# Four edits in a two-layer hybrid encoder: matmul order in the state-space mixer, a sum of squares on VectorE, and the order of the final norm

## The reference, cut to what matters

```python
def mamba2_mixer(h, in_proj, conv_w, conv_b, dt_bias, a_log, d_skip, norm_w, out_proj):
    proj = h @ in_proj                       # z | x, B, C | dt
    z, xbc, dt_raw = ...
    xbc = silu(causal_dwconv(xbc, conv_w) + conv_b)
    xs, b_mat, c_mat = ...                   # 8 groups: x 256 wide, B and C 128 wide
    y = ssd_scan(xs, dt, a, b_mat, c_mat)    # needs C.B scores, decays, x * dt
    y = (y + d_skip * xs) * silu(z)
    yg = y.reshape(bsz, seq, 8, 256)
    yg = yg * rsqrt(mean(yg * yg, axis=-1, keepdims=True) + RMS_EPS)
    return (yg.reshape(bsz, seq, 2048) * norm_w) @ out_proj

# the end of the kernel
    return rmsnorm(h, final_norm)            # h * rsqrt(mean(h*h) + eps) * w
```

## Time and profile before

| | |
|---|---|
| median of three executions | 1324.3 us |
| the profiled execution | 1324.34 us |
| its span, first to last instruction or transfer | 1322.5 us |
| TensorE matmul busy | 1078.8 us, 82% |
| VectorE busy | 480.3 us, 36% |
| ScalarE busy | 239.7 us, 18% |
| HBM read | 459.38 MB, a mean of 348 GB/s over the span |
| chain that ended last | TensorE 54%, DMA 36%, VectorE 5% |

### The profile page before, as it was taken

One profiled execution on the slowest core, in us unless ns is written; L12 is line 12 of the kernel. 1 busy time (PEld: TensorE's weight loads), 2 busy tenths in 40 slices (PEclk: granted clock), 3 DMA queues, 4 the chain that ended last, 5 costly groups with the idle time before them and its releaser, 6 DMA issues.

```text
span 1322.5 us, 22258 instructions
## 1 busy us (share of the span) xinstructions
PE 1078.8 (82%) x9526; PEld 728.6 (55%) x9531; DVE 480.3 (36%) x1244; ACT 239.7 (18%) x539; POOL 7.8 (1%) x29
## 2 busy tenths in 40 slices
PE   8999888756897576889999999987866787768576
PEld 7888644433554243547888888854434353425243
DVE  2341563322232222236665556465322222213233
ACT  2220111111111111113433334121111111111111
POOL 1000000000000000000000000000000000000000
PEclk9999978878797787789999999998887879878788
DMA  9754799999999999994656663489999999999995
GB/s 341 222 251 191 283 428 425 426 426 428 425 428 425 425 428 426 426 368 137 215 189 224 215 207 143 160 358 427 425 428 425 427 426 424 427 427 427 426 426 238
DMA packets 90109, 461.95 MB, mean 349 GB/s; under 512 B 17180, under 2 KB 56344, under 8 KB 63384
## 3 DMA queue, kind: packets, MB, share of 16 engines
q1 hardware_dynamic: 89648, 460.34, 85.9%
q10 hardware_dynamic: 360, 0.15, 0.0%
HBM read 459.38 MB, written 1.08 MB: 348 GB/s over the span
## 4 chain that ended last, share of the span: by engine, by line
PE 54%; DMA 36%; DVE 5%; issue 2%; ACT 1%; SPq 1%; POOL 0%; POOLq 0%; DVEq 0%
DMA w_gu<-in_expert_w_up 19%; DMA w_x<-in_expert_w_up 17%; PE pb L1377 10%; PE pa L1377 7%; PE pa L1615 6%; PE wa L1615 6%; PE acc L1401 4%; PE pb L1606 4%; PE wb L1624 4%; PE acc L1503 2%; PE pb L1593 2%; PE acc L1634 1%; PE pb L1432 1%; ACT arena L511 1%; PE pb L1668 1%
## 5 line engine op out<-in xcount | busy, mean ns | idle before, releaser
L1615 PE MATMUL pa<-w_gu,arena 128*32 128x256 f32 x1408 | 114.2, 496 | 67.6 <-DMA w_gu<-in_expert_w_up 64.7
L1128 DVE TENSOR_SCALAR lower<-lower 128x128 f32<-128x128 f32 x64 | 14.4, 225 | 397.9 <-ACT lower L511 397.9
L1615 PEld LDWEIGHTS pa<-w_gu,arena 128*32 128x32 f32 x1408 | 55.2, 142 | 128.4 <-DMA w_gu<-in_expert_w_up 72.8
L1615 PE MATMUL wa<-w_gu,arena 128*32 128x256 f32 x1536 | 101.4, 423 | 29.7 <-DMA w_gu<-in_expert_w_up 29.7
L1377 PE MATMUL pb<-hnT,w_x 128*128 128x256 f32 x496 | 109.9, 380 | 2.4 <-DVE arena L1203 2.4
L511 ACT ACTIVATE arena<-wb 32x256 f32<-32x256 f32 (+2 forms) x248 | 93.5, 377 | 98.3 <-PE wb L1624 91.3
L1606 PE MATMUL pb<-arena,hs 128*128 128x128 f32 x480 | 78.9, 332 | 31.0 <-issue 18.0
L1377 PEld LDWEIGHTS pb<-hnT,w_x 128*128 128x128 f32 x496 | 93.4, 190 | 15.0 <-issue 2.8
L1606 PEld LDWEIGHTS pb<-arena,hs 128*128 128x128 f32 x480 | 72.7, 239 | 45.4 <-issue 44.5
L1615 PEld LDWEIGHTS wa<-w_gu,arena 128*32 128x32 f32 x1536 | 51.6, 122 | 79.6 <-DMA w_gu<-in_expert_w_up 37.5
L1593 PE MATMUL pb<-arena 32*128 32x512 f32 x128 | 75.2, 668 | 14.7 <-DVE arena L1024 11.3
(11 more groups left out here) (332 smaller groups left out, 1300.7 us busy)
## 6 DMA issues: line engine op xcount, KB each, us to landing
w_gu<-in_expert_w_gate SPq DMA_DIRECT2D x44, 2048.0 KB, 31.9
w_gu<-in_expert_w_up SPq DMA_DIRECT2D x44, 2048.0 KB, 36.6
w_dn<-in_expert_w_down SPq DMA_DIRECT2D x32, 2048.0 KB, 41.1
w_x<-in_expert_w_gate SPq DMA_DIRECT2D x20, 2048.0 KB, 32.8
w_x<-in_expert_w_up SPq DMA_DIRECT2D x20, 2048.0 KB, 37.6
arena<-in_expert_w_down SPq DMA_DIRECT2D x16, 2048.0 KB, 38.1
hnT<-in_expert_w_down SPq DMA_DIRECT2D x16, 1024.0 KB, 36.5
arena<-in_expert_w_down SPq DMA_DIRECT2D x16, 1024.0 KB, 40.1
```

Of the source, the lines that this page charges most:

```text
L1128: link(v.tensor_scalar(eg, eg, 1.0, None, ALU.add))
L1615: ins = mm(gu[32 * j:32 * j + 32, :, :], xb[:, k, c0:c0 + CAP], w_gu[s][:, :, k, P * j:P * j + P], start=(k == 0), stop=(k == KC - 1))
```

## The change

1. **Order in units 0 and 1.** `odd_bc(g + 2)` stands right behind `odd_y(g)`, ahead of `odd_x(g + 1)`, for g = 0 and 1. From unit 2 on it stays behind `odd_ss(g)`.
2. **Order in the last unit.** In unit 7 `odd_z` stands ahead of `odd_scores`.
3. **Squares.** VectorE adds the two halves of the squares (128x256) in every unit, and `odd_ss` is one matmul, not two.
4. **Final norm.** VectorE multiplies the second half of the first tile by the norm's weights without the inverse root; ScalarE multiplies it by the inverse root afterwards, and that part is stored first. The mean of the second tile is formed ahead of the first scaling.

```diff
@@ SyncE, the stores
-            for n, (t, i) in enumerate(norm_parts()):
-                sp_.wait_ge(S["y_ready"], n + 1)
+            for t, i, sem, n in ((0, 1, "sum_sq", 2 * TT + 1), (0, 0, "y_ready", 2), (1, 0, "y_ready", 3), (1, 1, "y_ready", 4)):
+                sp_.wait_ge(S[sem], n)
@@ ScalarE, behind the four squares
+            act.wait_ge(S["y_ready"], 1)
+            act.wait_ge(S["rstd"], TT + NORMS - 1)
+            af(y_out[:, 0, 512:], y_out[:, 0, 512:], ACT.Copy, scale=st[:, 4, 0:1]).then_inc(S["sum_sq"], 1)
@@ VectorE, odd_gate
-                v.tensor_tensor(sq, yz, yz, ALU.mult).then_inc(S["yz_done"], 1)
+                link(v.tensor_tensor(sq, yz, yz, ALU.mult))
+                v.tensor_tensor(sq[:, 0, :], sq[:, 0, :], sq[:, 1, :], ALU.add).then_inc(S["yz_done"], 1)
@@ VectorE, the end
             mean_square(0)
             dve.wait_ge(S["fnorm_in"], 16)
-            dve.wait_ge(S["rstd"], TT + 4)
+            v.tensor_tensor(y_out[:, 0, 512:], h[:, 0, 512:], fnorm[:, 512:], ALU.mult).then_inc(S["y_ready"], 1)
+            mean_square(1)
+            dve.wait_ge(S["rstd"], TT + NORMS - 1)
             normed(0, 0)
-            mean_square(1)
-            normed(0, 1)
-            dve.wait_ge(S["rstd"], TT + 5)
+            dve.wait_ge(S["rstd"], TT + NORMS)
             normed(1, 0)
             normed(1, 1)
@@ TensorE, odd_ss
-                for j in range(2):
-                    ins = mm(wb[:, 0:SEQ], ones[:, :], sq[:, j, :], start=(j == 0), stop=(j == 1))
-                ins.then_inc(S["yss_done"], 1)
+                mm(wb[:, 0:SEQ], ones[:, :], sq[:, 0, :], start=True, stop=True).then_inc(S["yss_done"], 1)
@@ TensorE, the units
-                odd_scores(g)
-                odd_z(g)
+                if g == ODD_UNITS - 1:
+                    odd_z(g)
+                    odd_scores(g)
+                else:
+                    odd_scores(g)
+                    odd_z(g)
                 odd_y(g)
+                if g < 2:
+                    odd_bc(g + 2)
...
-                if g + 2 < ODD_UNITS:
+                if 2 <= g < ODD_UNITS - 2:
                     odd_bc(g + 2)
```

## The result

The changed kernel takes 1341.18 us (median of 4 executions, 1339.76 to 1341.88) against 1324.39 us for the kernel before (4 executions, 1322.28 to 1325.58). The ratio is 1.0128, with a 95% interval of 1.0116 to 1.0140: it is slower, by 16.8 us. Predicted were 1339.2 us, in a range of 1332.5 to 1343.5. The profiled execution took 1340.69 us with a span of 1338.9 us, 16.4 us more than before.

The account below looks back on a forecast made before the run. TensorE was taken to bound mixer C and the weight stream the experts, so mixer time delays the end. 10.0 + 4.0 - 1.7 + 1.5 + 1.7 - 0.6 = +14.9 us on 1324.34 gave 1339.2 us, range 1332.5 to 1343.5.

Parts of the forecast that it names:

- What bounds: TensorE bounds mixer C, the weight stream layer 1's experts; a microsecond more in mixer C ends the kernel a microsecond later.
- Edit 1, +10.0: Units 0 and 1: B/C no longer covers the silu of x, so scores start 7.0 us behind x; +10.0 us.
- The clock, +4.0: Behind the two 6.6 us gaps in mixer C TensorE's clock falls: 2.0 us twice, +4.0, bounds 2.6 and 6.0.
- the ten waits that I had read: TensorE waits of 2.9 to 8.3 us, all losing clock time behind them: 1.3 to 3.0 us, on average 2.0.
- Edit 2, +1.5 and +1.7: Unit 7: z no longer covers VectorE's inputs, +1.5 us; clock behind the 3.4 us gap, +1.7, bounds 0 and 3.0.
- Edit 3, -1.7: Units 2 to 5: one matmul pair of the squares goes, 4 x 0.43 us; VectorE's addition is covered; -1.7 us.
- Edit 4, -0.6: Final norm: the last two scalings end at about 1319.5 instead of 1320.06 us; -0.6 us, between 0 and -1.0.
- The queues at 0: SyncE's four transfers leaving together at about 647 us cost nothing; if late, up to 3 us.

Follow-up runs that it names:

- e1: Kernel before with only B/C ahead of x in units 0 and 1: 1340.31 us against 1323.64, ratio 1.0126.
- e11: Kernel before plus VectorE squares, unit 7 reordered with cover, 2 of 16 B/C matmuls ahead of x (units 0, 1), silu before mix (units 1, 2): 1320.04 us, 0.9968.
- e6: Changed kernel plus 28 unused matmuls of zeros behind the squares of units 0 and 1, filling TensorE's waits: 1334.53 us, ratio 1.0082 to the kernel before.
- e2: Kernel before with only z ahead of the scores in unit 7: 1328.19 us, ratio 1.0038.
- e7: Changed kernel, but z ahead of scores in units 1 and 2, not 7; unit 0's output projection ahead of unit 2's outputs: 1332.15 us, ratio 1.0060 to before.

## Why the prediction was right, point by point

- **What bounds.** Right. +16.5 us between the scores of unit 0 and the first load became +16.4 us in the span; the stream's own length, 0.7 us more, kept within its scatter.
- **Edit 1, +10.0.** Right, in size and cause. From scores to scores, unit 0 went from 26.07 to 30.96 us (653.84 less 622.88), unit 1 from 25.83 to 33.22 (687.06 less 653.84), of which 2.3 are clock. e1 alone has the loss, and e11 shows the other side: a part of B/C may stand ahead of x as far as the rest still covers the silu, which e11 also moved forward.
- **The clock, +4.0.** Right in kind, too small in size: 5.1 us in the changed kernel, within the bounds of 2.6 and 6.0. e6 takes it away and gets 4.9 us back. The mean of the ten waits that I had read was too low for these two; they read 2.3 and 2.8.
- **Edit 2, +1.5 and +1.7.** The outputs start 17.0 us behind x(7) (849.75 less 832.73), as computed. The clock of this one wait is a matter of the execution: 1.6 us in the changed kernel, 0 in e2. That the +1.7 was met in the profile of the changed kernel is in part luck.
- **Edit 3, -1.7.** It fits the sum of the changed kernel; alone it gives 3.2 us, since there the squares of units 0 and 1 do not fall into a wait.
- **Edit 4, -0.6.** Near in the span (0.4), but partly by luck: by errors that went against each other. I had the first root at its old 0.55 us and the second at 1.00. The first now takes 0.95, beside VectorE's product, and the second 0.55, beside the first scaling, so the last scaling came 1.2 us earlier and not 0.6. What I had put at nothing was the end of the stores, and it cost 0.8 (3.2 less 2.4 us behind the last scaling). The chain of the changed kernel there:

```profile
1332.66 0.95 POOL st L502
1333.60 0.02 issue
1333.63 0.75 DVE w_x L1354
```

The rule that I cited from the Trainium skill ("SBUF — State Buffer", "Who interferes with whom") also says who waits: a VectorE operation with two inputs from memory and a GpSimd operation that reads there use a shared port pair, and whichever issues first holds off the other. The traces agree with it for GpSimd. The product started 0.17 us ahead of the first root, as the old scaling started 0.17 us ahead of the old second root (1.00 us), and the new second root, which started just ahead of the scaling, has its 0.55. For VectorE they do not show it: the scaling beside the second root took 0.75 us, and the one of the kernel before that had no root beside it also 0.75. The prediction had it that by this rule the new second root would not get the 0.55; it started first, and did. The first root, to which I had not applied the rule, was the long one. No run moves the product alone, so this cause is argued from the order of the starts.

- **The queues at 0.** Right: SyncE sent the four transfers one behind the other from about 647 us, and none of them released a wait of TensorE.

Between the profiled executions (+16.4 us) and the forecast (+14.9) lie 1.5 us: 1.0 in the clock, 0.2 in the norm and 0.7 in the scatter of the stream, less 0.4 ahead of the scores of unit 0. The median lies another 0.5 us above the profiled execution.

## What to carry to other kernels

Before moving a step into an idle slot, ask what it hides where it stands. Here 1.2 us of idle time were filled with a step that hid 7.0 us of another engine's chain, where 2 of its 16 matmuls, with the silu taken earlier, filled most of it (e11). The waits of 3.3 to 6.5 us on TensorE cost again behind their end, 1.5 to 2.8 us each in all profiled cases but one, as the matmuls there ran at the lower clock at first; and a step that moves also takes along its own waits, as z did in e7.

## What the runs showed of the hardware

Behind waits of 6.54 us between stretches with TensorE full, the granted clock fell as it did among the experts (0.71 and 0.65 over the 8 us behind them). Behind a wait of 3.26 us ahead of the outputs of unit 7 it fell in three profiled executions (0.80, 0.81, 0.79 over 8 us) and did not in a fourth (1.00). The fall can also come behind the end of a wait: in e7, after the wait of 3.27 us, TensorE was busy at a clock of 0.99 for 1.2 us, and then stood at 0.50 for 3.4 us. With matmuls of zeros in the wait the clock stayed at 1.00 in both waits of e6. And a GpSimd operation on 128 single values took 0.55 us, but 0.93 to 0.95 when a VectorE product of two tensors had started just ahead of it, and 1.00 when a scaling of two tensors had: the same in all thirteen profiles, six with the new order of the norm (first root long, second short) and seven with the old one (first short, second long).
